# Stick-breaking queries, keys and values projected by token rows in 512-column item pairs

## What is computed

```
dn_qkv, dn_z, dn_b, dn_a, sb_q, sb_k, sb_v, gate_a, gate_b = split_cols(h @ w_in)
o_a = gated_delta_rule_chunked(l2norm(q), l2norm(k), v, g, beta)      # from conv + silu of dn_qkv
y_a = (rmsnorm(o_a, dn_out_norm) * silu(dn_z)) @ w_branch_a
qb, kb, vb = rmsnorm(sb_q), rmsnorm(sb_k), sb_v                       # per head of 128
z = qb @ kb.T * scale                                                 # stick-breaking attention
log_1mb = where(causal, -softplus(z), 0)
survive = reverse_cumsum(log_1mb) - log_1mb
o_b = where(causal, exp(log_sigmoid(z) + survive), 0) @ vb
y_b = o_b @ w_branch_b
return (sigmoid(gate_a) * y_a + sigmoid(gate_b) * y_b) @ w_out
```

## Time and profile before

| | us |
|---|---|
| median of 3 runs | 2599.41 (2598.93 to 2600.7) |
| the profiled execution's own time | 2599.58 |
| its span in the profile | 2597.7 |
| PE busy | 2586.5 |
| DVE busy | 2028.6 |
| ACT busy | 1544.6 |
| the stretch that changes, layer 0 (281.86 to 422.74 us) | 140.88 |
| the same in layer 1 (974.99 to 1115.80 us) | 140.81 |

### The profile page before, as it was taken

The page is one execution under the profiler, slowest core; times in us unless marked ns, Lnnn a source line. Parts: engine busy times, 40 slices in busy tenths (PEclk is TensorE's granted clock), DMA queues, the critical chain, the costliest instruction groups (busy, mean ns, idle before and its releaser), DMA issues.

```text
span 2597.7 us, 34900 instructions
## 1 busy us (share of the span) xinstructions
PE 2586.5 (100%) x14184; PEld 2211.3 (85%) x14184; DVE 2028.6 (78%) x2078; ACT 1544.6 (59%) x1703; POOL 121.4 (5%) x148
## 2 busy tenths in 40 slices
PE   9999999999999999999999999999999999999999
PEld 7889998888888899888888889978888889988887
DVE  8887754698799686557998995676997996677987
ACT  6556774465565567645656555555656555655654
POOL 0000170000000004400000000000000000000000
PEclk9999999999999999999999999999999999999999
DMA  8646444466465555545747465544755646544662
GB/s 260 227 152 214 155 155 170 145 227 225 150 230 173 171 164 166 178 143 178 237 164 233 161 204 181 161 146 154 243 195 188 209 162 189 161 146 148 215 229 105
DMA packets 354876, 475.03 MB, mean 183 GB/s; under 512 B 28758, under 2 KB 279966, under 8 KB 354462
## 3 DMA queue, kind: packets, MB, share of 16 engines
q1 hardware_dynamic: 349246, 469.86, 55.1%
q10 hardware_dynamic: 4416, 1.90, 0.3%
q0 software_dynamic: 1056, 1.05, 0.3%
HBM read 467.13 MB, written 5.64 MB: 182 GB/s over the span
## 4 chain that ended last, share of the span: by engine, by line
PE 97%; ACT 1%; DVE 1%; DMA 0%; SPq 0%; issue 0%; DVEq 0%; ACTq 0%
PE bank L421 29%; PE bank L423 29%; PE bank L422 29%; PE bank L1020 1%; PE bank L565 1%; PE bank L1909 1%; PE bank L1885 1%; DMA raw<-in_ffn_w_in 0%; PE bank L2790 0%; PE bank L2737 0%; PE bank L2726 0%; ACT w_hi L402 0%; PE bank L1833 0%; PE bank L1832 0%; PE bank L1856 0%; PE bank L2747 0%
## 5 line engine op out<-in xcount | busy, mean ns | idle before, releaser
L421 PE MATMUL bank<-w_hi,xn_hi 128*128 128x512 f32 (+2 forms) x1856 | 704.4, 380 | 1.4 <-DVE xn_lo L537 0.8
L423 PE MATMUL bank<-w_hi,xn_lo 128*128 128x512 f32 (+2 forms) x1856 | 691.9, 373 | 0.0
L422 PE MATMUL bank<-w_lo,xn_hi 128*128 128x512 f32 (+2 forms) x1856 | 691.0, 372 | 0.0
L408 DVE TENSOR_TENSOR w_lo<-raw,w_hi 128x2048 fp32r<-128x2048 f32 (+2 forms) x190 | 411.6, 2168 | 217.3 <-ACT w_hi L402 216.7
L1157 ACT ACTIVATE w_hi<-raw 128x2048 fp32r<-128x2048 f32 x192 | 367.3, 1913 | 135.6 <-DMA raw<-in_ffn_w_out 39.7
L402 ACT ACTIVATE w_hi<-raw 128x2048 fp32r<-128x2048 f32 (+2 forms) x198 | 358.0, 1809 | 147.8 <-PE bank L423 146.6
L1265 DVE TENSOR_TENSOR w_lo<-raw,w_hi 128x2048 fp32r<-128x2048 f32 x192 | 438.4, 2284 | 1.0 <-ACT w_hi L1157 0.9
L421 PEld LDWEIGHTS bank<-w_hi,xn_hi 128*128 128x128 f32 x1856 | 349.7, 188 | 64.5 <-issue 5.2
L423 PEld LDWEIGHTS bank<-w_hi,xn_lo 128*128 128x128 f32 x1856 | 349.5, 188 | 61.3
L422 PEld LDWEIGHTS bank<-w_lo,xn_hi 128*128 128x128 f32 x1856 | 350.0, 189 | 56.4
L421 PE MATMUL bank<-w_hi,hid_hi 128*128 128x512 f32 x704 | 278.1, 395 | 0.0
(11 more groups left out here) (404 smaller groups left out, 3922.8 us busy)
## 6 DMA issues: line engine op xcount, KB each, us to landing
raw<-in_w_in SPq DMA_DIRECT2D x122, 1024.0 KB, 5.2
raw<-in_ffn_w_in SPq DMA_DIRECT2D x126, 512.0 KB, 5.4
raw<-in_ffn_w_out SPq DMA_DIRECT2D x44, 1024.0 KB, 5.2
raw<-in_ffn_w_down SPq DMA_DIRECT2D x44, 1024.0 KB, 5.2
raw<-in_ffn_w_gate SPq DMA_DIRECT2D x64, 512.0 KB, 4.3
raw<-in_ffn_w_up SPq DMA_DIRECT2D x64, 512.0 KB, 5.3
block<-in_ffn_w_in SPq DMA_DIRECT2D x48, 512.0 KB, 7.6
block<-in_ffn_w_gate SPq DMA_DIRECT2D x24, 512.0 KB, 6.6
```

The lines of the kernel that those rows point to most:

```text
L408: dve.tensor_tensor(in_order(kind, slot, w_lo), as_loaded(kind, slot), in_order(kind, slot, w_hi).bitcast(F32), ALU.subtract).then_inc(s_l ...
L421: pe.matmul(out, a_hi, b_hi, start=start, stop=False, skip_group_check=check)
L422: pe.matmul(out, a_hi, b_lo, start=False, stop=False, skip_group_check=check)
L423: return pe.matmul(out, a_lo, b_hi, start=False, stop=stop, skip_group_check=check)
```

## The change

The list of items from 15 on becomes, in pairs: `svr` (15, 16), `sbq` (17, 18), `sbk` (19, 20), `sbq` (21, 22), `sbk` (23, 24), `svr` (25, 26), `gb` (27 to 30), `z` (31, 32), `b` (33 to 36), `ga` (37 to 40). A query or key pair has 512 columns, four heads; its first item holds the upper half of the rows, its second the lower, and each item does 12 matmuls of 512 columns for the first tokens (t = 0) and 12 for the second (t = 1). The norm chain runs twice for a pair, once for each half of the tokens, during the pair's second item and behind it. PE turns the first half in the middle of the next item and the second half at its end. The three banks 0, 1 and 2 are given to the pairs by `PAIR_BANKS`. The stick parts hang on `STICK` = (22, 23, 27, 28): scores at the end of that item, logs 1 item later, sums 2, out 3, `ob_hi` and `ob_lo` 4.

```
-        + [("sbq", 4112), ("sbk", 5136), ("sbq", 4368), ("sbk", 5392), ("svr", (6160, 0)), ("svr", (6160, 1)),
-           ("sbq", 4624), ("sbk", 5648), ("sbq", 4880), ("sbk", 5904), ("svr", (6672, 0)), ("svr", (6672, 1))]
-        + [("gb", (8208 + 512 * n, h)) for n in range(2) for h in range(2)] + [("b", (512 * n, h)) for n in range(2) for h in range(2)]
-        + [("z", (3584, h)) for h in range(2)] + [("ga", (7184 + 512 * n, h)) for n in range(2) for h in range(2)] + [("a", (0, 0))])
+        + [(kind, (at + 512 * n, h)) for kind, at, n in (("svr", 6160, 0), ("sbq", 4112, 0), ("sbk", 5136, 0),
+                                                         ("sbq", 4112, 1), ("sbk", 5136, 1), ("svr", 6160, 1)) for h in range(2)]
+        + [("gb", (8208 + 512 * n, h)) for n in range(2) for h in range(2)] + [("z", (3584, h)) for h in range(2)]
+        + [("b", (512 * n, h)) for n in range(2) for h in range(2)] + [("ga", (7184 + 512 * n, h)) for n in range(2) for h in range(2)]
+        + [("a", (0, 0))])
...
-        BY_PAIRS = ("gb", "b", "z", "ga")
+        BY_PAIRS = ("svr", "sbq", "sbk", "gb", "b", "z", "ga")
...
+        PAIR_BANKS = ((0, 1), (0, 1), (2, 0), (1, 2), (0, 1), (2, 0)) + ((1, 0),) * (len(PAIRS) - 6)
+        SB = [j for j in PAIRS if KINDS1[j] in ("sbq", "sbk")]
+        STICK = (22, 23, 27, 28)
...
         def wait_pair_bank(pe, l, j, t):
-            if j > PAIR0:
-                wait_read(pe, l, j - 2 + t)
+            b = pair_banks(j)[t]
+            for i in range(PAIRS.index(j + 1) - 1, -1, -1):
+                if b in PAIR_BANKS[i]:
+                    wait_read(pe, l, PAIRS[i] - 1 + PAIR_BANKS[i].index(b))
+                    return
+            if b < 2:
+                wait_read(pe, l, max(i for i in range(PAIR0) if bank1(i) == b))
...
 mixer1_pe:
+                        if j - 1 in SB and t == 0:
+                            turn_sb_pe(pe, l, 2 * SB.index(j - 1))
...
                 for r in range(4):
-                    if j == SBK[r] + 5:
+                    if j == STICK[r] + 3:
                         stick_out_pe(pe, l, r)
-                    if j == SBK[r] + 4:
+                    if j == STICK[r] + 2:
                         stick_sums_pe(pe, l, r)
-                    if j == SBK[r] + 2:
+                    if j == STICK[r]:
                         stick_scores_pe(pe, l, r)
...
+                if j - 1 in SB:
+                    turn_sb_pe(pe, l, 2 * SB.index(j - 1) + 1)
...
 mixer1_act:
+            def sb_norms(j, t):
+                n = 2 * SB.index(j) + t
+                act.activation(sb_sq[:, :, :], b4[pair_banks(j)[t]], ACT.Square).then_inc(s_sbsq, 1)
+                act.wait_ge(s_sbss, l * 8 + (n + 1))
+                if n:
+                    act.wait_ge(s_readv, l * READ_DVE + n)
+                act.activation(sb_root[:, :], sb_ss[:, :], ACT.Sqrt, bias=eps_col[:, 1:2]).then_inc(s_sbroot, 1)
...
 mixer1_dve:
+                if j in SB:
+                    sb_sums_dve(dve, l, 2 * SB.index(j))
...
                 if 1 <= j <= LATE and j != GATES_ACT:
                     split_lo(dve, pm, j + 2)
...
+                if j in SB:
+                    sb_scale_dve(dve, l, j, 0)
+                    sb_sums_dve(dve, l, 2 * SB.index(j) + 1)
+                    sb_scale_dve(dve, l, j, 1)
+                if j - 1 in SB:
+                    sb_ready_dve(dve, l, 2 * SB.index(j - 1))
```

More of the change, by code:

```diff
@@ L463, in by_weight_rows @@
                              kc == 0, kc == KC - 1, True)
-            return mm
[L466 to L473, removed]
             return mm
@@ L1482, in build @@
         sb_sq = put("sb_squares", [4, P], at=shared + 51200)
-        sb_tok = [put(f"sb_tokens{r}", [NT, 256], at=shared + 49152 + 4096 * r) for r in range(2)]
+        sb_tok = [put(f"sb_tokens{r}", [4, P], at=shared + 49152 + 4096 * r) for r in range(2)]
         Mi = put("l_t", [NT, HEADS, P], at=shared + 57344)
@@ L1737, in mixer1_pe @@
                     mm = features(pe, slot, pair[bank1(j)][0:16, :, :], xn_hi, xn_lo, n=16, m=16)
-                elif kind == "svr":
-                    by_weight_rows(pe, slot, bank[bank1(j)][:, :], MIX1[j][1][1], 1)
-                    mm = by_weight_rows(pe, slot, bank[2][:, :], MIX1[j][1][1], 0)
-                elif kind in ("sbq", "sbk"):
-                    mm = tokens(pe, slot, pair[bank1(j)], xn_hi, xn_lo)
                 elif kind in BY_PAIRS:
@@ L1747, in mixer1_pe @@
                             wait_pair_bank(pe, l, j, t)
-                        mm = by_weight_rows(pe, slot, bank[t][:, :], h, t, *((ob_hi, ob_lo) if kind == "b" else (xn_hi, xn_lo)))
+                        mm = by_weight_rows(pe, slot, bank[pair_banks(j)[t]][:, :], h, t,
+                                            *((ob_hi, ob_lo) if kind == "b" else (xn_hi, xn_lo)))
                         if h == 1 and t == 0:
                             mm.then_inc(s_pair, 1)
+                        if j - 1 in SB and t == 0:
+                            turn_sb_pe(pe, l, 2 * SB.index(j - 1))
                 else:
@@ L1853, in turn_sb_pe @@
                 pe.wait_ge(s_la, l * 4 + 2)
-            for h in range(2):
-                for t in range(NT):
-                    mm = pe.transpose(b4[5][:, 2 * h + t, :], sb_tok[n % 2][:, t, P * h:P * h + P], ident)
+            for h in range(4):
+                mm = pe.transpose(b4[5][:, h, :], sb_tok[n % 2][:, h, :], ident)
             mm.then_inc(s_sbt, 1)
@@ L2024, in mixer1_act, with take_pair @@
                               ).then_inc(s_zero, 16)
-            def take_pair(kind, column, t):
-                n = (column - {"gb": 8208, "z": 3072, "ga": 7184}[kind]) // 512
-                dst, func = {"gb": (gate_b, ACT.Copy), "z": (zs, ACT.Silu), "ga": (gate_a, ACT.Sigmoid)}[kind]
-                act.activation(dst[:, t, half(n)], bank[t][:, :], func).then_inc(s_read, 1)
+            def take_pair(j, kind, column, t):
+                n = (column - {"svr": 6160, "gb": 8208, "z": 3072, "ga": 7184}[kind]) // 512
+                dst, func = {"svr": (sv, ACT.Copy), "gb": (gate_b, ACT.Copy), "z": (zs, ACT.Silu), "ga": (gate_a, ACT.Sigmoid)}[kind]
+                act.activation(dst[:, t, half(n)], bank[pair_banks(j)[t]][:, :], func).then_inc(s_read, 1)
+            def sb_norms(j, t):
[5 more added lines that the diff above has]
+                act.activation(sb_root[:, :], sb_ss[:, :], ACT.Sqrt, bias=eps_col[:, 1:2]).then_inc(s_sbroot, 1)
             def silu(j):
@@ L2268, in mixer1_dve @@
                             dve.wait_ge(s_used, pm.base + (j + 1 + START))
-                        dve.tensor_tensor(gate_b[:, t, part_b], bank[t][:, :], gate_b[:, t, part_b],
+                        dve.tensor_tensor(gate_b[:, t, part_b], bank[pair_banks(j)[t]][:, :], gate_b[:, t, part_b],
                                           ALU.mult).then_inc(s_readv, 1)
```

92 lines of the change are left out of this document (34 added, 58 removed).

## The result

The changed kernel takes 2650.08 us (median of 6 runs, 2646.4 to 2650.27), the kernel before 2599.63 (6 runs). The ratio is 1.019, with a 95% interval of 1.0177 to 1.0203. It is slower, as forecast, but the time is 20 us above the forecast and 9 above the range.

A forecast was written before the change was run, and what follows sets the result against it. The prediction took PE as the bound, busy 2586.5 of 2597.7 us. Waits of 34.4 us, -4.2 for PE work and +0.4 for breaks cost 30.6 us on 2599.6, giving 2630.2 us; range 2621 to 2641.

The forecast's parts named there:

- PE's work: Eight items per layer switch to 512-column matmuls: 4.2 us less in both layers, 0.4 us back for more breaks.
- The waits: New PE waits in items 15 to 31: 17.2 us per layer, 34.4 us in both layers.
- item 15, convolution: Item 15 now writes bank 0 and must wait for item 14's convolution: PE waits 0.9 us.
- item 23, bank 5: Pair at item 22: DVE empties bank 5 only after softplus and split, so PE waits 4.8 us.
- item 30, `ob_lo`: `delta_pe` step 2 needs the third stick part's `ob_lo`, behind ACT's split and sigmoid: PE waits 4.2 us.
- item 31, `ob_lo`: Step 3 needs the fourth stick part's `ob_lo`, behind the splits of item 34: PE waits 3.9 us.
- The chain of the norm: ACT and DVE steps from a pair's second item until bank 5 is empty; 1.7 us waits at items 19 and 21.
- item 24: Pair at item 24: bank 5 empty at 32.8, PE asks at 35.9, so no wait.
- the clock: PE's clock in the long waits: the sum included no cost for a fall, leaving it to a rival.
- rival 1: PE's clock falls in the long waits, 2.2 us each, one to six falls: 2632 to 2643 us; chance 0.22.
- Rival 2: Waits are not on PE; only PE's work and item 15's 0.9 us count: 2597.6 us; chance 0.03.
- Rivals 3 and 4: One long wait shorter, 2614.0 or 2620.6 us (0.08); more waits in items 26 to 36, above 2643 (0.04).

The follow-up runs named there:

- The last kernel: Changed kernel with bank 5 emptied first, late stick parts an item earlier, item 24's first norm before the logs, the change's banks kept: 2597.41 us.
- the kernel kept busy: Changed kernel with matmuls of zeros into a free bank filling the five long PE waits of each layer: 2629.89 us, ratio 1.0117.

## Why the prediction was wrong

**PE's work** was right. The last kernel has all of the change's matmuls and only the wait on the convolution; it is 2.4 us faster than before, and the one without that wait 3.8, which is the forecast's -4.2 + 0.4. The stretch agrees: 140.88 - 138.95 = 1.9 us in layer 0. By the formula in the Trainium skill ("TensorE: Matmul & The Clock Gate", the back-to-back issue gap) the gain would have been 1.0 us, an estimate; here the measurement decides for the rows. The section gives that formula for a single matmul and says that a stream of weight loads and matmuls, which this kernel is, departs from it; the forecast left that out.

**The waits** were right, each by its place and its releaser, and within 0.4 us by size (in us):

| wait in each layer | forecast | measured |
|---|---|---|
| item 15, convolution | 0.9 | 0.74 |
| item 19, bank 5 | 1.7 | 1.62 |
| item 21, bank 5 | 1.7 | 1.9 |
| item 23, bank 5 | 4.8 | 4.75, 4.83 |
| item 30, `ob_lo` | 4.2 | 3.84 |
| item 31, `ob_lo` | 3.9 | 3.84 |
| both layers | 34.4 | 33.5 |

The chain of the norm, whose steps all came from rows of the kernel before, held to 0.2 us at every turn. That DVE empties bank 5 only behind its split is what it rests on, and taking that away took all six waits away. The forecast's statement that item 24 leads to no wait was right only because PE came late: without the earlier waits it has one. That the kernel kept busy comes within 0.3 us of 2630.2 is luck in part, since the waits were put 0.9 us too high in sum.

**The step that failed is the clock.** The sum put it at nothing and left its fall to rival 1, at a chance of 0.22 and for one to six of the long waits. The runs showed the fall in place of that zero: seven stretches at 0.50, 37.5 us in all, cost 16.7 us in the profiled execution, and 20.2 us by the medians. Each of the six runs shows it, at a mean clock of 0.991 or 0.992; in the trace of the kernel kept busy the clock is low only at the end of the program. The sum without the clock, 2630.2, is the time of that kernel (2629.89). Of the step three parts can be told apart, and the first and the third were wrong.

First, the evidence. The earlier trace rows show the clock at 1.00 for 4.2 us behind the last matmul, and the waits were of that size or a little more, so I took them for a doubtful case. But the clock did not keep that distance: in the changed kernel it fell 2.3 to 4.9 us after PE had stopped. In layer 0 the waits began at 350.1, 413.1 and 429.7, and the low stretches at 354.99, 416.43 and 433.49. Nor did it fall only while PE stood. The low stretches begin up to 1.0 us ahead of PE's restart (1133.23, restart at 1134.23) and up to 0.4 us behind it (1051.31, restart at 1050.88). So a clock that is still granted while PE stands says nothing of the clock that it gets when it starts. The Trainium skill (the same page, HAM oscillation) says that the next group after an idle gap of a few microseconds starts cold. The trace agrees behind all six waits of 3.8 us and more and behind one of 1.9 us, and in the kernel kept busy, which has no such gap, nothing fell. I had this sentence and weighed it below a row that did not show its case.

Second, the price, which was about right. I put 2.2 us on a fall, half of 4.3 us. The low stretches are 3.4 or 6.8 us long, 5.4 in the mean, and a fall cost 2.3 us in the mean.

Third, the number. I allowed for up to six, behind waits of 3.9 us and more. All six of those came, and a wait of 1.91 us in layer 1 was enough for a seventh, in PE's timeline:

```profile
1050.88 0.69 PE L1844 MATMUL bank<-consts,sb_tokens 128*128 128x128 f32 x4 [1.91 <-DVE sb_kT L2373]
1051.26 0.74 PE L422 MATMUL bank<-w_hi,xn_hi 128*128 128x512 f32 x1
...
1052.23 0.63 PE L424 MATMUL bank<-w_hi,xn_lo 128*128 128x512 f32 x1
1052.66 0.63 PE L422 MATMUL bank<-w_hi,xn_hi 128*128 128x512 f32 x1
```

The same wait in layer 0 (1.92 us at 334.93) had none. With seven falls at the forecast's own 2.2 us the sum is 2630.2 + 15.4 = 2645.6, against 2646.4 for the profiled execution.

**Rival 2** did not happen in the changed kernel. Its number did, once the waits were gone: it gave 2597.6 us for a kernel with none but the convolution's, and that kernel took 2597.41. **Rivals 3 and 4** did not happen: no wait is missing, and none was added behind item 31.

**What stays open.** The profiled execution of the changed kernel is 3.7 us faster than the median, and the mean clock of the four runs of 2650 us is 0.991 against its 0.992. Those means are rounded. At 0.991 a run has 45 to 50 us of low clock, the end of the program included; the profiled one (0.9924 in its trace) has 40. At 0.44 of its length the 5 to 10 us more would cost 2 to 5 us. That is an estimate, since only one execution has a trace; where the other runs fell is not known. Why the clock falls behind one wait of 1.9 us and not behind another of the same length was not found.
